# Hybrid decoder step: the prompts' output projection taken apart from the samples'

## Reference

```python
proj = rms_norm(x, norm1_g) @ w_in                  # pooling, short convolution, q/k/v, forget gate
y_pool, y_conv = causal_pool_mix(...), h_b * causal_dwconv(h_c * h_x, ...)
y_att = attn_fn(q, k, v, logf)                      # 8 heads of 128; samples read the paged cache
mix = concat([rms_norm(y_pool, g_pool), rms_norm(y_conv, g_conv), rms_norm(y_att, g_att)])
x = x + mix @ w_o                                   # w_o is 2048 x 2048: the output projection
a, gate = split(rms_norm(x, norm2_g) @ w_up)
x = x + (silu(causal_dwconv(a) + b) * gate) @ w_down
```

## Time and profile before

| what | value |
|---|---|
| time, median of 3 executions | 2919.9 us (2908.23 to 2923.85) |
| time of the profiled execution | 2925.93 us |
| its span, first to last instruction | 2924.0 us |
| PE busy | 2670.7 us (91% of the span), 20166 matmul records |
| DVE busy | 1438.6 us (49%) |
| ACT busy | 724.5 us (25%) |
| mean granted TensorE clock | 0.935 |

### The profile page before, as it was taken

How to read it: one execution, slowest core, us unless ns; L and a number is a source line. 1 busy time by engine, 2 the same in 40 slices (tenths; PEclk the granted TensorE clock), 3 DMA queues, 4 the chain that set the end, 5 groups by cost and what they waited for, 6 DMA issues and landing times.

```text
span 2924.0 us, 51472 instructions
## 1 busy us (share of the span) xinstructions
PE 2670.7 (91%) x20166; PEld 2364.6 (81%) x20166; DVE 1438.6 (49%) x5637; ACT 724.5 (25%) x963; POOL 18.3 (1%) x57
## 2 busy tenths in 40 slices
PE   5999999996677785998999999999999999999998
PEld 3897777784122332998999999999999999999998
DVE  4885556566966723434443434343443434343433
ACT  4321111111222224223322221222222222222221
POOL 0000000000000000000000000000000000000000
PEclk7999999998776777999999999999999999999999
DMA  6789989999999963333222233222233222232221
GB/s 236 251 294 357 330 323 335 352 335 364 344 364 368 350 217 109 121 102 102 87 87 87 87 102 101 87 87 87 87 105 98 87 87 87 88 107 95 87 87 62
DMA packets 270038, 522.50 MB, mean 179 GB/s; under 512 B 14218, under 2 KB 175595, under 8 KB 269252
## 3 DMA queue, kind: packets, MB, share of 16 engines
q1 hardware_dynamic: 247517, 487.37, 47.0%
q10 hardware_dynamic: 20247, 25.73, 2.5%
q0 software_dynamic: 2032, 6.13, 0.5%
HBM read 495.55 MB, written 24.05 MB: 178 GB/s over the span
## 4 chain that ended last, share of the span: by engine, by line
PE 75%; DMA 10%; DVE 6%; SPq 4%; issue 2%; ACT 2%; POOL 0%; ACTq 0%; DVEq 0%; POOLq 0%
PE ps L627 74%; DMA t_r<-in_cache_v 7%; DVE t_work L1579 3%; SPq L530 2%; DMA t_r<-in_cache_k 2%; SPq L528 1%; DMA t_wraw<-in_w_in 1%; PE ps L630 1%; ACT t_wh L1057 1%; DVE t_wl L1418 1%; SPq L517 0%; DVE t_xl L1418 0%; DVE t_auxW L1418 0%; ACT t_xh L1057 0%; DMA t_auxW<-in_pool_w 0%
## 5 line engine op out<-in xcount | busy, mean ns | idle before, releaser
L627 PE MATMUL ps<-t_xh,t_wh 128*128 128x260 f32 x4608 | 948.2, 286 | 44.1 <-DVE t_xl L1418 42.3
L627 PE MATMUL ps<-t_xh,t_wl 128*128 128x260 f32 x4608 | 938.7, 284 | 0.0
L627 PE MATMUL ps<-t_xl,t_wh 128*128 128x260 f32 x4608 | 937.8, 284 | 0.0
L1418 DVE TENSOR_TENSOR t_wl<-t_wraw,t_wh 128x1024 fp32r<-128x1024 f32 x376 | 460.2, 1225 | 908.7 <-ACT t_wh L1057 908.5
L1057 ACT ACTIVATE t_wh<-t_wraw 128x1024 fp32r<-128x1024 f32 x376 | 398.0, 1059 | 1626.2 <-PE ps L627 1626.2
L627 PEld LDWEIGHTS ps<-t_xh,t_wh 128*128 128x128 f32 x4608 | 718.7, 190 | 98.4 <-issue 52.3
L627 PEld LDWEIGHTS ps<-t_xh,t_wl 128*128 128x128 f32 x4608 | 718.3, 190 | 0.0
L627 PEld LDWEIGHTS ps<-t_xl,t_wh 128*128 128x128 f32 x4608 | 717.4, 190 | 0.0
L1579 DVE CUSTOM_DVE_ANT_0 t_work<-t_r,t_work 128x128 f32<-128x128 f32 x2048 | 455.0, 287 | 100.4 <-DMA t_r<-in_cache_k 89.8
L627 PE MATMUL ps<-t_r,t_pr 128*8 128x512 f32 x1024 | 219.6, 692 | 130.1 <-DMA t_r<-in_cache_v 126.1
L627 PE MATMUL ps<-t_hh,t_wh 128*128 128x260 f32 x1408 | 285.3, 284 | 3.4 <-issue 3.4
(11 more groups left out here) (234 smaller groups left out, 1115.5 us busy)
## 6 DMA issues: line engine op xcount, KB each, us to landing
t_r<-in_cache_k SPq DMA_DIRECT2D x256, 512.0 KB, 8.0
t_r<-in_cache_v SPq DMA_DIRECT2D x256, 512.0 KB, 7.3
t_wraw<-in_w_up SPq DMA_DIRECT2D x44, 2048.0 KB, 8.0
t_wraw<-in_w_in SPq DMA_DIRECT2D x22, 2048.0 KB, 8.7
t_wraw<-in_w_down SPq DMA_DIRECT2D x22, 2048.0 KB, 7.9
t_wraw<-in_w_o SPq DMA_DIRECT2D x8, 2048.0 KB, 11.9
scr_proj<-t_stg ACTq DMA_DIRECT2D x40, 256.0 KB, 4.8
t_aux<-scr_proj ACTq DMA_DIRECT2D x8, 768.0 KB, 12.4
```

Source lines behind the costliest of these rows:

```text
L627: return pe.matmul(out, lhsT, rhs, start=start, stop=stop)
L1418: return dve.tensor_tensor(out, in0, in1, op)
```

## The change

The output projection becomes part of the slots, from `OUT0` = `TAIL` + 3 = 152, one chunk per slot (`out_chunk`). It multiplies the prompts' 512 columns alone, one matmul where there were two of 260, and in the first two chunks PE waits for each block of `kt` by itself. The samples' projection is done in float32 with the samples as the loaded operand, 8 columns wide: `sample_out` takes `kt` 0 to 7 from the raw weights in `wraw` after every fourth chunk (8 matmuls of 256), `sample_out_columns` turns the result back (2 matmuls), and `sample_out_attention` takes `kt` 8 to 15 (4 times 8 matmuls of 512) inside the first FFN tiles. For these, rows 8 to 15 of `w_o` are loaded a second time. The first FFN tiles go over all 16 blocks four times, half by half and tile by tile, instead of once with 12 matmuls per block; the samples' half is last. Residuals are loaded at `TAIL`, and the last two blocks of them behind `x_lo`. The samples' steps are put between the slots. The scores and exponentials stay in `Eb`, and the `Exp` no longer waits for the value pages; `page_slots` gives two value pages per slot everywhere. Since the layout before ends at slot 148, one short of `TAIL`, both tables put the same pages in the same slots.

```diff
-            rate = 4 if at >= TAIL else 2
+            rate = 2
...
-SLOTS = max(V_END[-1] + 3, TAIL + 9)
+OUT0 = TAIL + 3
+OUT_CHUNKS = 32
+SLOTS = OUT0 + OUT_CHUNKS
+LAST = V_END[-1]
...
@@ SP
+                if R_O + 2 <= n <= R_F + 1:
+                    sp.wait_ge(ws_full, n - R_O - 1)
...
+                n, late = divmod(s - OUT0 + 7, 4)
+                if late == 0 and 2 <= n < 8:
+                    load_raw(R_O + n, n % 2, w_o_v, 2 * n * P)
...
+            sp.wait_ge(w_lo, 4 * R_F + 4)
+            sp.dma_start(wraw[:, 0, :].rearrange("p (k n) -> p k n", k=2), out_rows(12)).then_inc(w_loaded[0], 16)
+            sp.wait_ge(y_norm, Y_O1)
+            sp.dma_start(wraw[:, 1, :].rearrange("p (k n) -> p k n", k=2), out_rows(14)).then_inc(w_loaded[1], 16)
...
@@ PE
+            def out_chunk(c):
...
+                for k in range(8):
+                    kt = 8 * half + k
+                    if c < 2:
+                        pe.wait_ge(x_lo, kt + 1)
...
+                    for w, x in ((block_h, xh), (block_h, xl), (block_l, xh)):
+                        last = mm(ps[:, 2 * u, :], w, x[:, kt, 0:SEQ], kt == 0 and w is block_h and x is xh,
+                                  kt == KT - 1 and w is block_l)
+                last.then_inc(w_used, 1)
+
+            def sample_out(n):
...
+                for k in range(8):
+                    lane = 32 * (k % 4)
+                    last = mm(ps[lane:lane + DEC, 5, 0:256], gS[:, k * DEC:(k + 1) * DEC],
+                              wraw[:, n % 2, 256 * k:256 * (k + 1)], k < 4, k >= 4)
...
+            def sample_out_columns(n):
+                pe.wait_ge(ws_kept, n + 1)
+                for j in range(2):
+                    at = (2 * n + j) * DEC
+                    last = mm(ps[:, 6, at:at + DEC], wtmp[:, j * P:(j + 1) * P], lane8[:, :])
...
+            def sample_out_attention(k0, rows):
+
+                for k in (k0, k0 + 1):
+                    for c in range(4):
+                        last = mm(ps[32 * c:32 * c + DEC, 5, :], gS[:, k * DEC:(k + 1) * DEC], rows(k - k0, c),
+                                  k == 8, k == KT - 1)
...
+                if s >= OUT0:
+                    c = s - OUT0
+                    out_chunk(c)
+                    if c % 4 == 1:
+                        sample_out(c // 4)
+                    if c % 4 == 3:
+                        sample_out_columns(c // 4)
...
-            first_tiles(4 * R_F, T_FF // 2 + 1, 16, (0, 1))
+            first_ffn_tiles(4 * R_F)
...
@@ ACT
+                    if group == 1 and t == 12:
+                        act.wait_ge(y_norm, Y_O3)
+                        copy(osb, ps[:, 5, :]).then_inc(y_norm, 1)
...
-                    if r:
-                        act.wait_ge(v_used, r * PAGES + PRIME)
-                    act.activation(pr[:, :, :], shifts, ACT.Exp).then_inc(c_p, 1)
+                    probs = Eb[:, r * PAGES:(r + 1) * PAGES, :]
+                    act.activation(probs, probs, ACT.Exp).then_inc(c_p, 1)
...
@@ DVE
+            def out_tile(t):
+                u = t % 2
+                dve.wait_ge(w_used, 4 + CHUNKS + 2 * t + 2)
+                dve.wait_ge(res_loaded, 64)
+                tt(x2(t), ps[:, 2 * u, :], x2(t), ALU.add).then_inc(acc_free[u], 1)
```

More of the change, by code:

```diff
@@ L69, in page_slots @@
         while done < PAGES:
-            rate = 4 if at >= TAIL else 2
+            rate = 2
             take = min(rate, PAGES - done)
-            values[at] = [r * PAGES + done + i for i in range(take)]
+            if take:
+                values[at] = [r * PAGES + done + i for i in range(take)]
             done += take
@@ L662, in norm @@
                 pe.wait_ge(n_sum, norm_first[group] + hi - lo)
-                for c in range(2):
-                    last = mm(ps[:, norm_bank[group] + c, 0:HALF], ones[:, :], sumsq[group][:, c * HALF:(c + 1) * HALF])
+                for c in range(2 if group == 0 else 1):
+                    w = HALF if group == 0 else SEQ
+                    last = mm(ps[:, 4 + c, 0:w], ones[:, :], sumsq[group][:, c * w:(c + 1) * w])
                 last.then_inc(n_full, 1)
@@ L1162, in _, with rstd64 @@
             act.activation(fn, fn, ACT.Ln, bias=1.0).then_inc(f_soft, 1)
-            def rstd64(summed, done):
-                act.wait_ge(summed, 1)
+            def rstd64(summed, value, done):
+                act.wait_ge(summed, value)
                 v = sm[:, :, :].rearrange("p h b -> p (h b)")
@@ L1325, in _ @@
                     mix_rstds((2,))
[L1326 to L1334 removed]
+                if s == TAIL:
+                    for n in range(2):
+                        for b in range(2):
+                            act.wait_ge(h_stored[n][b], 16 * 4)
@@ new lines, in _ @@
+                if TAIL <= s < TAIL + 2:
+                    head(0, CHUNKS + 2 * (s - TAIL))
+                    head(0, CHUNKS + 2 * (s - TAIL) + 1)
+                if s == TAIL + 1:
+                    act.wait_ge(y_norm, Y_RED)
+                    act.activation(rsS[:, 0:2, :], rsS[:, 0:2, :], ACT.Ln, bias=epsc[:, :], scale=1.0 / 512).then_inc(y_norm, 1)
+                    act.wait_ge(y_norm, Y_LOG)
+                    act.activation(rsS[:, 0:2, :], rsS[:, 0:2, :], ACT.Exp, scale=-0.5).then_inc(y_norm, 1)
@@ new lines, in _ @@
+                if TAIL + 1 <= s < TAIL + 5:
+                    for t in range(4 * (s - TAIL - 1), 4 * (s - TAIL)):
+                        mix_head(t)
+                if s >= OUT0:
+                    c = s - OUT0
+                    head(0, CHUNKS + c + 4)
+                    if c % 2 == 0 and c >= 2:
+                        out_square(c // 2 - 1)
+                    if c % 4 == 2:
+                        n = c // 4
+                        act.wait_ge(ws_full, n + 1)
+                        if n:
+                            act.wait_ge(ws_tr, n)
+                        copy(wtmp, ps[:, 5, 0:256]).then_inc(ws_kept, 1)
@@ L1458, in norm @@
                 n0 = norm_first[group]
+                w = T if group == 0 else SEQ
                 dve.wait_ge(n_rb, group + 1)
@@ new lines, in sample_squares, with sample_sums @@
+            def sample_squares(lo, hi):
+                tt(sq3[:, lo:hi], yS[:, lo:hi], yS[:, lo:hi], ALU.mult).then_inc(y_norm, 1)
+                tt(g3[:, lo:hi], yS[:, lo:hi],
+                   par[:, GO + lo:GO + hi].unsqueeze(2).broadcast_to([P, hi - lo, DEC]), ALU.mult)
+            def sample_sums(g0, g1, full):
+                dve.wait_ge(y_norm, full)
+                for g in range(g0, g1):
+                    lo, hi, _ = mix_groups[g]
+                    last = dve.tensor_reduce(rsS[:, g, :], ps[:, 3, lo * DEC:hi * DEC].rearrange("p (k b) -> p b k", b=DEC),
+                                             AX.X, ALU.add)
+                last.then_inc(y_norm, 1)
@@ new lines, in _ @@
+                if s >= OUT0:
+                    c = s - OUT0
+                    weight_rest(0, CHUNKS + c + 4)
+                    if c % 2 and c >= 3:
+                        out_sum(c // 2 - 1)
+                    if c % 2:
+                        out_tile(c // 2)
+                if s == LAST + 2:
+                    sample_mix()
+                    sample_squares(8, 16)
+                if s == LAST + 3:
+                    sample_sums(2, 3, YA_TOT)
+                if s == LAST + 4:
+                    sample_scale(2, 3, YA_RS)
```

368 lines of the change are left out of this document (220 added, 148 removed).

## The result

The changed kernel takes **2943.8 us** (median of 5 runs, 2933.2 to 2945.9), the kernel before 2921.6 beside it (median of 5, 2908.2 to 2929.9). The ratio is 1.0074, 95% interval 1.0040 to 1.0108: slower by 0.74%, some 22 us. The forecast was 2933, with 2918 to 2946 as its range; 22 us lost where it had 13.4.

The account below looks back on a forecast made before the run. PE was taken as the bound (busy 91%, under 75% of the last-ending chain). Terms of -4.6 us to the projection's end and +18 in the first FFN tiles gave +13.4 and, from the 2919.9 median, 2933 us; range 2918 to 2946.

Parts of the forecast that it names:

- Before `TAIL`: Stages ahead of the output projection: same page tables, and the wait for value pages stays with the copy; 0 us.
- Start of the projection: Output projection's first chunks: last block normed at about 1185.2, chunk 1 done at 1185.9; 3.2 us won.
- Wide matmuls: Other 30 projection chunks: 720 matmuls of 512 columns replace 1440 of 260; about 17 us won.
- Samples' matmuls: In the projection: eight times 1.2 us for the samples' matmuls, seven times 0.75 for turning back; 14.9 us lost.
- Residual: First residual in the projection: its last transfer lands late behind a weight transfer; 1 us lost, bounds 0 and 3.4.
- Sum to the projection's end: Terms for start, wide matmuls, samples' matmuls and residual added up to the end of the output projection: -4.6 us.
- Gap: Wait of 12.3 us between projection and first FFN matmul, for the second norm: same chain, 0 us.
- First FFN tiles: First FFN pass at the second norm's pace, with samples' matmuls, then three more passes: 18 us lost, bounds 15.1 to 21.
- wide matmuls keep the 11.7 ns and the paced pass runs at half clock: Rival, 17%: projection's wide matmuls win 10.8 us, first FFN tiles lose 21; 2947, or 2940 at half.
- No slower, since the start is early: Rival, 17%: small steps hide beside the blocks' pairs, chunk 1 is done at 1174, 12 us won: 2921.
- Long matmuls overlap: Rival, 2%: a 512-column projection matmul costs no more than one of 260, 86 us saved instead of 17: 2864.
- the freed `Exp`: Rival, 4%: the exponential releases value pages at three ends of a sequence's pages, 3.64 us each: 2922.

Follow-up runs that it names:

- e7: The kernel before with the value stage's scores and exponentials written in place, the exponential not waiting for the value pages: ratio 1.0003 to the kernel before.
- e4: Not the layer: a loop of PE matmuls alone over widths and operand kinds; 512 columns took 227 ns in rounded float32, 215 in bfloat16.
- e11: Not the layer: 512-column rounded float32 matmuls in the changed kernel's pattern; 226 ns with one moving block, 234 with 16 in turn, 232 with the kernel's pattern.
- e2: The changed kernel without the samples' matmuls between the output projection's chunks: 214.0 us to the projection's end against 227.4.
- e5: The changed kernel with six matmuls per second-norm block, samples' blocks earlier, last residual asked for earlier: 2936.6 us, ratio 1.0053 to the kernel before.
- e1: The changed kernel with the prompts' wide projection matmuls cut into two of 256 columns: 227.8 us to the projection's end against 227.4.
- e3: The changed kernel with the samples' matmuls for blocks 8 to 11 moved ahead of the second norm: first FFN tiles 47.0 us against 46.5.
- e8: The changed kernel without the samples' matmuls in the first FFN tiles: those tiles 43.2 us against 46.5.
- e9: e5 without the samples' matmuls in the first FFN tiles: those tiles 37.6 us against 41.6.

## Why the forecast came out as it did

Slower was forecast and slower it is, with the largest loss in the place that was named; its size was 22.2 and not 13.4 us up to the fifth chunk. One term is off by 12.0 us, more than the whole difference of 8.8; that the time still fell into the range owes something to luck, since the start and the samples' matmuls came out 5.0 us better than forecast. The chances were no clear call either: 45% for a time above 2934.5, 49% for one too near to tell.

- **Before `TAIL`, 0:** right (e7). What varies there varies by itself: the square that serves as a mark stands between 1121.5 and 1150.1 us in the eleven profiles, and every kernel's time scatters with it; the seven of the changed layout lie within the spread of the four of the old one.
- **Start of the projection, -3.2:** chunk 1 is done 46.0 us behind the mark (1169.94), where the forecast had 48.0; the last block is normed at 43.9, where it had 47.3. Before, the 97th matmul, the first behind the same work, stands at

```profile
1189.65 0.28 PE L627 MATMUL ps<-t_xh,t_wh 128*128 128x260 f32 x1
```

  51.8 behind the mark, half a microsecond later than the forecast's 1189.1. So -5.8: right in kind, 2.6 better.
- **Wide matmuls, -17.3: this step failed.** The reasoning was that a long matmul hides its weight load and so takes its cycles and 3 ns. From 1169.94 to 1351.37 lie 181.4 us; without the samples' 12.5 and the wait of 1.06 they are 167.9, 233 ns for each of 720. Before, the same work took 1362.78 - 1189.65 = 173.1. The saving is 5.3 us, below even the bound of 10.8, which kept an excess of 11.7 ns for each matmul; the forecast's own sign of being wrong, starts 225 ns apart, is passed. The runs show three layers in the 233: 215 for bfloat16, which is what the forecast had in mind; 227 for rounded float32, so that the excess seen at 260 columns stays with a long matmul and goes with the operands' kind, be it by the moving operand or by the weight load (e4); and 232 with the blocks in turn (e11). The row that the forecast leaned on, is of plain float32 with its 1024 cycles. The Trainium skill, "TensorE: Matmul & The Clock Gate", "Back-to-back issue gap", has about 216 ns for an isolated matmul of 512 columns; the bfloat16 rows of e4 agree (215), the rounded ones don't (227). Its 131 ns for a sustained stream does not appear in any run, with 192 matmuls in a row of either kind.
- **Samples' matmuls, +14.9:** 12.5 (e2, less the shorter wait); the wide ones cost what was forecast, the turning back 0.44 us a time and not 0.75. **Residual, +1:** 1.06 us of idle time, 1.3 won when it is asked for earlier (e5). It hangs by little: e1 and e3, which ask as late, show no such wait.
- **Sum to the projection's end, -4.6:** -5.8 - 5.3 + 12.5 + 1.1 = +2.5, as measured.
- **Gap, 0:** -0.3 (it is 12.2 us before, where the prediction writes 12.3).
- **First FFN tiles, +18:** +20.0, inside its bounds of 15.1 to 21 (+22.7 by e1's profile). The passes at the norm's pace are as described; the square of e5, e8 and e9 shows what they are made of. What the forecast did not see as one cause: the split of the columns into halves is forced by the samples' late norm. And the low clock that it had only as a bound is there: windows of PE after, over the end of the first pass and the start of the second,

```profile
1386.00:1391.00 5.00, 3.99 (x27) 0.64 1.10 349
1391.00:1396.00 5.00, 5.00 (x30) 0.68 0.74 238
1396.00:1401.00 5.00, 5.00 (x44) 1.00 0.00 0
```

  and in e8, whose first pass of three matmuls a block is left without the samples' work,

```profile
1386.00:1391.00 5.00, 3.62 (x13) 0.50 1.10 348
1391.00:1396.00 5.00, 5.00 (x31) 0.50 0.82 258
```

  the lower of the two levels for the whole pass and past it. In the changed kernel's second pass 44 records go by in 5 us at the upper level (from 1396) and 30 in the window before, so that window alone costs 1.6 us.

Of the rivals, "wide matmuls keep the 11.7 ns and the paced pass runs at half clock", with 2940 to 2947, is nearer to what happened (2943.8) than the sum. Its first half is even too mild; its second gave 21 us for the tiles, which took 20.0 more. It came near also because it had the start and the residual too dear (1 us won and 3.4 lost, where 5.8 and 1.06 were measured). "No slower, since the start is early" needed the last block before 1172, 34.1 us behind the mark; it came at 43.9 (1167.84). "Long matmuls overlap" and "the freed `Exp`" are refuted by e4 and e7.

## What to carry to other kernels

Take the price of an operation that the trace lacks from rows of the same kind of operand, and let an excess that those rows show stand (here 12 ns over the cycles at 260 columns, 14 to 20 at 512) unless a row shows it gone; a bound set by the same excess is no bound. Columns of another batch that ride along in a matmul's width are almost free (118 ns for 260 columns, 119 for 256 in e4); taken out, they need their own matmuls (12.5 us), here their own norm stands in the way of half the columns (4.2 us, and then 13.1 of matmuls that no longer hide behind anything), and they break up the work that filled another engine's pace. And look for the part of a change that wins by itself: the early start alone wins 4.8 us in a stage where the whole change loses 22.2.

## What the runs showed of the hardware

- Matmuls on rounded float32 at the upper clock, alone on the core and from one moving block: 227 ns for 512 columns, 173 for 384, 118 for 260, 119 for 256, 111 for 128. From 512 to 256 columns the time falls by 108 ns, from 256 to 128 by 8. Bfloat16 takes 215 for 512 (e4).
- With 16 moving blocks in turn 512 columns take 232 to 234; transfers of 255 GB/s, DVE and ACT beside them cost nothing, the same 303 records in 70 us (e11).
- In e8 the granted clock read 0.50, the lower level, all through the pass that waits for a block before each three matmuls, and in the window of full work from 1391 to 1396.
- The same instructions in the first FFN tiles took 46.5 us in the changed kernel's profile and 49.2 in e1's, whose clock read 0.50 where the other's read 0.64 to 0.68.
